# A hybrid decoder layer with a mixture of experts: a sixth expert buffer in shared tensors, the first experts' rows by dense one-hot products, and a new order of the front, the small products, the logits and the last loads

## The chip, the core and the metric

The kernel runs on one core of one Trainium2 chip. The engines used are TensorE (PE, matrix products; PEld is its weight load), VectorE (DVE), ScalarE (ACT), GpSimd (POOL) and SyncE (SP, which only issues transfers here). SBUF is the on-chip memory of 128 partitions, PSUM the eight accumulation banks that PE writes. The metric is the device time of one execution, in microseconds; the median of three runs is given, and one more execution was profiled.

## What is computed

One layer for 256 prompt tokens and 8 sequences of 8 sample tokens (320 tokens, D = 1024), all in fp32:

```python
xn = rmsnorm(x, norm1);  proj = xn @ w_in                      # 1024 x 7456
lru_x, lru_y, rw, gate_lru, gate_rwkv = split(proj)
out_lru  = rglru(causal_conv(lru_x)) * gelu(lru_y)
out_rwkv = rwkv7(rw, ...)                                      # 16 heads of 64
x = x + (sigmoid(gate_lru)*out_lru + sigmoid(gate_rwkv)*out_rwkv) @ w_out
t = rmsnorm(x, norm2)
g = argmax(t @ rg + rgb); two best of the 8 experts in group g # 32 experts
y = sum over the two: weight * (silu(t @ wg[e]) * (t @ wu[e])) @ wd[e]
out = rmsnorm(x + y, final_norm)
```

Each expert has three matrices of 1 MiB (gate, up, down: 1024 x 256 and 256 x 1024), so the experts' weights are 96 MiB. The states (convolution, LRU, token shift, WKV) are outputs too.

## The kernel before

Every engine has its own instruction stream, written out by hand; a wait on a counting semaphore stands wherever one engine needs another. There is no scheduler: the order on each engine is that of the code. The program has four stages.

**Front (0 to 65 us).** SP loads x, the states and the first weights; ACT issues 13 small vector loads into `vrows` (L1103), then squares and roots for the first norm. PE waits for all 13, transposes them (L582), transposes the states (`strows`, `shrows`, `murows`, 36 small transposes, L585 to L589), then the normed rows `xn` (24 transposes, L599, two banks in turn) and makes three products of the shared columns (L605). DVE scales the rows (L1402) and applies `norm1` by column (L1408).

**Pairs of heads (65 to 549 us).** `turn(i, ...)` runs eight times, six of them in a loop, once for each pair of heads (128 channels). The big projections are `proj` (L627); between them stand many small products of 64 rows or 64 columns: `own` (L667, L669), the transposes `turned` (L649: a plain product with the identity for the lower half, a transpose for the upper half), the samples' transposes (L697 to L705) and the levels of a triangular inverse (L738, L745). PE's last product of the first half of `proj(.. "r" ..)` waits for the DVE's first transposed level (`lvX`) and for ACT's copies (`tm`).

**Output projection and routing (549 to 619 us).** `out(t)` for three token tiles (L914), `x2(t)` transposes the rows normed with `norm2` (L932, L924), `logits(t)` (L956) multiplies by the router. DVE picks the experts (L1717 to L1784), PE counts places with triangular products (L972 to L977), DVE builds the one-hot `disp` for experts 0 and 1, and PE gathers their columns directly: for each of 8 chunks of D, `xn2` as weights and `disp` as moving operand (L983, L985). The rows of the other experts go through DRAM: `xn2d` is written by ACT's queue and gathered by POOL with indirect transfers (L533, L535).

**Experts (619 to 872 us) and the end.** For each expert e PE runs `up(e)` (`GU`, L1008, 64 slots), the transposes of the next rows (L1002), `dn(e-1)` (`DN`, L1015) and `turn_h(e)` (L1037). DVE copies the result to `ye`, POOL scatters it to `ybuf` in DRAM (L539). The weights go through five buffers, carved out of tensors whose earlier use has ended, so SP's loads wait: gate and up of experts 0 to 3, down of 0 go at once; down of 1 and gate and up of 4 after `out(2)` (`wo_ps` 3, since they lie over the weights of `out`); down of 3 after the logits; down of 2 and 4 after the first rows' products (`gT_ps` 2). From expert 5 on, SP waits for `gu >= e-4`, loads gate and up of e, waits for `dn >= e-4`, loads down of e. At the end SP loads the two choices of every token back from `ybuf` (`ya`, L505 to L509), DVE adds them with their weights (`combine`, L1840, L1841), and the last norm (ACT L1302, L1304, DVE L1704) is stored.

## Time and profile before

| | us |
|---|---|
| median of 3 runs | 897.65 (894.34 to 900.71) |
| profiled execution, its own time | 895.88 |
| its span | 894.1 |
| PE busy | 812.1 (91%) |
| DVE busy | 457.0 (51%) |
| ACT busy | 248.7 (28%) |
| moved by the DMA engines | 159.85 MB |

The page cuts the span in 40 slices of 22.35 us. Through the front and the pairs PE is at nine tenths and the DMA engines are mostly idle. From slice 25 on (559 us) the DMA engines run at nine tenths and about 390 GB/s, except in slice 27 (604 to 626 us), where they move 119 GB/s; TensorE's granted clock is down to a half in the same place. The chain that ended last is 70% PE, 10% transfers and 8% DVE.

### The profile page before, as it was taken

To read this page: it belongs to the slowest core of one execution; us is meant where nothing else is said; L and a number is where in the kernel's file an instruction comes from. 1 tells how busy PE (TensorE), PEld (TensorE's weight loads), DVE (VectorE), ACT (ScalarE), POOL (GpSimd) and SP (SyncE) were. 2 spreads that over 40 slices of the span, in tenths; PEclk is the share of its full clock that TensorE was granted. 3 is DMA by queue.
4 is the path that set the end of the run, shared out by engine and by line. 5 is a ranking of instruction groups with operands and counts; after the bars stand their busy time and mean duration, and the time that the engine had idled before them with its cause. 6 is when DMAs were issued, how large, how long until landed. Compare 5 with 4: busy or idle time off the path is not lost.

```text
span 894.1 us, 16251 instructions
## 1 busy us (share of the span) xinstructions
PE 812.1 (91%) x6152; PEld 510.3 (57%) x6152; DVE 457.0 (51%) x1065; ACT 248.7 (28%) x584; POOL 64.8 (7%) x72
## 2 busy tenths in 40 slices
PE   3999999999999999999999989979899988888780
PEld 3566666666666666666666655456555544445440
DVE  1376687686686786886875936143221111111114
ACT  4123342351441432433423523220111111111112
POOL 1000000000000000000000000000322222222110
PEclk9999999999999999999999999975999999999995
DMA  9252060060250140320600512993999999999955
GB/s 221 78 134 73 25 167 15 25 170 8 58 144 23 45 134 23 105 73 23 166 12 23 165 30 60 375 413 119 344 386 387 385 396 391 392 392 388 399 203 180
DMA packets 114225, 159.85 MB, mean 179 GB/s; under 512 B 27470, under 2 KB 91528, under 8 KB 105974
## 3 DMA queue, kind: packets, MB, share of 16 engines
q1 hardware_dynamic: 98180, 149.14, 48.6%
q0 software_dynamic: 5136, 6.04, 2.5%
q10 hardware_dynamic: 10867, 4.09, 1.9%
q8 instruction: 29, 0.48, 0.2%
q14 instruction: 13, 0.11, 0.0%
HBM read 155.99 MB, written 13.64 MB: 190 GB/s over the span
## 4 chain that ended last, share of the span: by engine, by line
PE 70%; DMA 10%; DVE 8%; SPq 7%; issue 3%; ACT 1%; ACTq 1%; DVEq 0%; POOLq 0%
PE bank L627 17%; PE bank L1008 7%; SPq L457 5%; PE bank L633 4%; PE bank L914 4%; PE bank L795 4%; PE bank L1015 3%; PE bank L858 3%; DMA scratch<-in_exp_up 3%; DMA wall<-in_exp_up 3%; PE bank L738 3%; DMA vecs<-in_exp_up 2%; PE bank L649 2%; PE bank L745 2%; DVE vecs L1465 2%
## 5 line engine op out<-in xcount | busy, mean ns | idle before, releaser
L627 PE MATMUL bank<-xnT,wall 128*128 128x320 f32 x656 | 195.3, 442 | 1.8 <-DVE wkv L1571 1.8
L627 PEld LDWEIGHTS bank<-xnT,wall 128*128 128x128 f32 x656 | 119.0, 190 | 51.5 <-DVE wkv L1571 5.4
L1813 DVE SCALAR_TENSOR_TENSOR vecs<-vecs,bank 128x128 f32<-128x128 f32 x32 | 9.2, 287 | 144.7 <-ACT vecs L1360 144.7
L1008 PE MATMUL bank<-vecs,scratch 128*64 128x256 f32 x448 | 56.5, 409 | 9.1 <-DMA vecs<-in_exp_up 8.2
L1008 PE MATMUL bank<-scratch 128*64 128x256 f32 x384 | 45.8, 393 | 11.8 <-DMA scratch<-in_exp_up 10.6
L1809 DVE COPY vecs<-bank 128x512 f32<-128x512 f32 x32 | 22.1, 691 | 58.1 <-PE bank L1015 42.3
L1008 PEld LDWEIGHTS bank<-vecs,scratch 128*64 128x64 f32 x448 | 33.5, 147 | 28.1 <-DMA vecs<-in_exp_up 9.6
L533 POOL DMA_INDIRECT merged<-xn2d,gidx x4 | 3.7, 918 | 622.5 <-DVE gidx L1791 621.6
L1360 ACT ACTIVATE vecs<-bank 128x128 f32<-128x128 f32 x32 | 8.9, 277 | 136.9 <-PE bank L1008 136.9
L795 PE MATMUL bank<-xnT,wall 128*128 128x320 f32 x128 | 43.9, 455 | 2.5 <-DVE wkv L1611 2.5
L1008 PEld LDWEIGHTS bank<-scratch 128*64 128x64 f32 x384 | 28.2, 141 | 25.9 <-DMA scratch<-in_exp_up 11.8
L1564 DVE TENSOR_TENSOR wkv<-bank,consts_sb 128x256 f32<-128x256 f32 (+1 forms) x40 | 18.1, 451 | 46.5 <-PE bank L738 46.5
L539 POOL DMA_INDIRECT ybuf<-vecs,sidx x32 | 32.1, 1004 | 77.6 <-DVE vecs L1809 76.9
L1002 PEld LDWEIGHTS bank<-consts_sb,merged 64*128 64x128 f32 x240 | 28.7, 200 | 12.0 <-issue 12.0
L858 PE MATMUL bank<-xnT,wall 128*128 128x320 f32 x112 | 33.1, 439 | 0.0
L1002 PE MATMUL bank<-consts_sb,merged 64*128 64x64 f32 x240 | 32.8, 277 | 0.0
L535 POOL DMA_INDIRECT merged<-xn2d,gidx x26 | 24.7, 949 | 108.0 <-PE bank L1002 104.8
L738 PEld LDWEIGHTS bank<-wkv,scratch 64*64 64x64 f32 x704 | 23.6, 134 | 14.7 <-issue 13.2
L914 PE MATMUL bank<-wall,merged 128*128 128x512 f32 (+1 forms) x84 | 30.7, 595 | 0.1
L738 PE MATMUL bank<-wkv,scratch 64*64 64x64 f32 x704 | 29.1, 224 | 0.9 <-DVE wkv L1571 0.9
L1008 PE MATMUL bank<-wall,scratch 128*64 128x256 f32 x192 | 23.7, 403 | 5.3 <-DMA wall<-in_exp_up 5.3
L795 PEld LDWEIGHTS bank<-xnT,wall 128*128 128x128 f32 x128 | 21.2, 190 | 10.8 <-DVE wkv L1611 4.8
(389 smaller groups left out, 1374.1 us busy)
## 6 DMA issues: line engine op xcount, KB each, us to landing
wall<-in_w_in SPq DMA_DIRECT2D x58, 512.0 KB, 5.6
vecs<-in_exp_gate SPq DMA_DIRECT2D x14, 1024.0 KB
vecs<-in_exp_up SPq DMA_DIRECT2D x14, 1024.0 KB
scratch<-in_exp_gate SPq DMA_DIRECT2D x12, 1024.0 KB
scratch<-in_exp_up SPq DMA_DIRECT2D x12, 1024.0 KB
scratch<-in_exp_down SPq DMA_DIRECT2D x7, 1024.0 KB
wall<-in_exp_down SPq DMA_DIRECT2D x7, 1024.0 KB
wall<-in_exp_gate SPq DMA_DIRECT2D x6, 1024.0 KB
```

What stands on the lines that cost most here:

```text
L457: sp.dma_start(wgu[b][:, g].rearrange("p k f -> p (k f)"), gu_src(name, e)).then_inc(S(f"ewg{b}"), 16)
L535: pool.indirect_dma_start(xg[j], None, xn2d, bass.IndirectOffsetOnAxis(ap=e, axis=0), bounds_check=last, oob_is_err=False).then_inc(S(sem) ...
L539: pool.indirect_dma_start(yhalf, bass.IndirectOffsetOnAxis(ap=e, axis=0), ye[:, b, :], None, bounds_check=4 * QROWS - 1, oob_is_err=False) ...
L627: q = mm(tpbank(L, name), wbuf[name][:, k, :], xnT[:, k, :], start=(k == 0), stop=(k == KC - 1))
L633: mm(tpbank(L, name), lhsT, rhs, start=True, stop=True).then_inc(S("tp"), 1)
L738: q = mm(bank[2][at64(e), 64 * u:64 * u + 64], am[at64(e), u, e, 0, :], X[at64(e), u, :], start=True, stop=True)
L795: q = mm(tpbank(L, "gr"), wbuf["gr"][:, k, :], xnT[:, k, :], start=(k == 0), stop=(k == KC - 1))
L858: q = mm(tpbank(L, "lx"), wbuf["lx"][:, k, :], xnT[:, k, :], start=(k == 0), stop=(k == KC - 1))
L914: q = mm(b, merged[:, k, t0:t0 + n], wo[k][:, 512 * h:512 * h + 512], start=(k == 0), stop=(k == KC - 1))
L1002: q = tr(b[:, CAP * k:CAP * k + CAP], src[:, k:D:KC], ident[r, r])
L1008: q = mm(b[64 * f:64 * f + 64, 0:256], xT[:, k, :], w[:, :, k, 128 * f:128 * f + 128], start=(k == 0), stop=(k == KC - 1))
L1015: q = mm(b[64 * d:64 * d + 64, :], hT[:, 64 * j:64 * j + 64], down(w, j, d), start=(j == 0), stop=(j == 1))
```

## The change

**Memory.** The small tensors that only the pairs of heads use (`s0raw`, `so_s`, `cvT`, `shT`, `w2a2`, `g2a`, `g2b`, `wxa`, the three `pad1`, `pad3`, `cacc`, `dif`) become slices of two tensors, `shared0` and `shared1`. After the last pair these hold gate and up of a sixth buffer. Its down matrix goes in three pieces to ends of `wall` and `wkv`. The gains of the last norm move to `scratch3` and are loaded when 28 experts' products are done.

**Loads.** Gate and up of expert 5 are issued before the wait for the first rows; `next_gu` runs one expert ahead of `next_dn`:

```diff
-            sp.dma_start(fnb, a["final_norm"].rearrange("(a d) -> a d", a=1).broadcast_to([P, D])).then_inc(S("fn_in"), 16)
-            sp.wait_ge(S("lg_ps"), 1)
+            sp.wait_ge(S("lg_ps"), 2)
             load_dn(3, 3)
+            sp.wait_ge(S("wkv_out"), 80 * PAIRS)
+            load_gu(5, 5)
             sp.wait_ge(S("xn2d"), 64)
-            sp.wait_ge(S("gT_ps"), 2)
+            sp.wait_ge(S("rows_ps"), 2)
             load_dn(2, 2)
             load_dn(4, 4)
...
-            for e in range(5, NE):
-                sp.wait_ge(S("gu"), e - 4)
-                load_gu(e % 5, e)
-                sp.wait_ge(S("dn"), e - 4)
-                load_dn(e % 5, e)
+            sp.wait_ge(S("rows_out"), 128)
+            load_dn(5, 5)
+            def next_gu(e):
+                sp.wait_ge(S("gu"), e - 5)
+                load_gu(e % 6, e)
+            def next_dn(e):
+                sp.wait_ge(S("dn"), e - 5)
+                load_dn(e % 6, e)
+            next_gu(6)
+            next_gu(7)
+            next_dn(6)
+            next_dn(7)
+            next_gu(8)
+            for e in range(9, NE):
+                next_gu(e)
+                next_dn(e - 1)
+            next_dn(NE - 1)
```

SyncE's expert loads from gate and up of expert 4 on, before ( `vecs`, `scratch`, `wall`, `xnT`, `wkv`, `merged` are the tensors that hold buffers):

```order
L457 DMA wall<-in_exp_gate 128x2048
L457 DMA wall<-in_exp_up 128x2048
L475 DMA wall<-in_final_norm 128x1024
L461 DMA xnT<-in_exp_down 128x2x1024
L461 DMA wkv<-in_exp_down 128x2x1024
L464 DMA wkv<-in_exp_down 128x1024
L464 DMA merged<-in_exp_down 128x512
L464 DMA xnT<-in_exp_down 128x512
L484 DMA wkv<-in_final_norm 64x512 x2
L457 DMA vecs<-in_exp_gate 128x2048
L457 DMA vecs<-in_exp_up 128x2048
L461 DMA scratch<-in_exp_down 128x2x1024
```

and the same place now:

```order
L491 DMA wall<-in_exp_gate 128x2048
L491 DMA wall<-in_exp_up 128x2048
L498 DMA xnT<-in_exp_down 128x2x1024
L494 DMA shared<-in_exp_gate 128x1024 x2
L494 DMA shared<-in_exp_up 128x1024 x2
L498 DMA wkv<-in_exp_down 128x2x1024
L501 DMA wkv<-in_exp_down 128x1024
L501 DMA merged<-in_exp_down 128x512
L501 DMA xnT<-in_exp_down 128x512
L501 DMA wall<-in_exp_down 128x1024
L501 DMA wkv<-in_exp_down 128x512 x2
L491 DMA vecs<-in_exp_gate 128x2048
```

The four pieces of expert 5 stand between down of 3 and down of 2, and 0.75 MiB of final gains is gone from here.

**First rows.** The rows of experts 0 and 1 are gathered as rows, with `disp` as weights and 512 columns of `xn2` moving, copied by ACT to `xg01`, and transposed:

```diff
-            for k in range(KC):
-                b, c = bank[0 if k < 4 else 3], 128 * (k % 4)
-                for t in range(2):
-                    mm(b[:, c:c + 128], xn2[:, t, k:D:KC], disp[:, t], start=(k % 4 == 0 and t == 0), stop=False, skip_group_check=True)
-                for h in range(2):
-                    q = mm(b[at64(h), c:c + 128], xn2h[at64(h), k:512:KC], disp[at64(h), 2], start=False, stop=True, skip_group_check=True)
+            for h in range(2):
+                b, c = bank[3 if h else 0], slice(512 * h, 512 * h + 512)
+                for t in range(2):
+                    mm(b[:], disp[:, t].rearrange("p e s -> p (e s)"), xn2[:, t, c], start=(t == 0), stop=False)
+                mm(b[:], disp[at64(h), 2].rearrange("p e s -> p (e s)"), xn2h[at64(h), :], start=False, stop=True).then_inc(S("rows_ps"), 1)
+            pe.wait_ge(S("rows_c"), 2)
+            for k in range(KC):
+                c = P * (k % 4)
+                q = tr(bank[1 if k < 4 else 4][:, c:c + P], xg01[:, k:D:KC], ident)
```

**Logits.** `norm2` is multiplied into the router's weights (`rw`), `x2` transposes `x1` itself, and DVE multiplies the logits by the inverse root afterwards. `logits(0)` and `logits(1)` stand around the second half of `out(2)`. TensorE from the third tile of `out` to the first expert's product, before:

```order
L914 MATMUL bank<-wall,merged 64x512 x14
L914 MATMUL bank<-vecs,merged 64x512 x2
L932 MATMUL bank<-consts_sb,wkv 128x128 x8
L939 MATMUL bank<-rowst,consts_sb 64x1 x2
L956 MATMUL bank<-rw,xnT 128x36 x8
L924 MATMUL bank<-consts_sb,wkv 128x128 x4
L956 MATMUL bank<-rw,xnT 128x36 x8
L956 MATMUL bank<-rw,xnT 64x36 x16
...
L983 MATMUL bank<-wkv 128x128 x2
L985 MATMUL bank<-wkv 64x128 x2
...
L1008 MATMUL bank<-vecs,scratch 64x256 x16
```

and now:

```order
L979 MATMUL bank<-wall,merged 64x512 x8
L998 MATMUL bank<-consts_sb,wkv 128x128 x8
L1023 MATMUL bank<-rw,xnT 128x36 x8
L979 MATMUL bank<-wall,merged 64x512 x6
L979 MATMUL bank<-vecs,merged 64x512 x2
L1023 MATMUL bank<-rw,xnT 128x36 x8
L990 MATMUL bank<-consts_sb,wkv 128x128 x4
...
L1051 MATMUL bank<-wkv 128x512 x2
L1052 MATMUL bank<-wkv 128x512
...
L1056 MATMUL bank<-consts_sb,merged 128x128 x8
L1080 MATMUL bank<-vecs,scratch 64x256 x16
```

Eight pairs of rows L983 and L985 became two pairs of L1051 and L1052 and eight transposes. The writes of `xn2d` are issued after the last root.

**Small products.** In `turn`, all of `own`'s first parts come first, then the quarter products grouped by bank; every `turned` is a plain product, in an order that alternates the output halves; the samples' transposes stand two products into `proj(.. "r" ..)`:

```diff
-                    for e in range(2):
-                        turned(b[at64(e), 128 * e:128 * e + 128], e, bk[:, 2 * j + e, 0], ident)
-                        turned(b[at64(1 - e), 128 * e:128 * e + 128], 1 - e, bk[:, 2 * j + e, 1], ident)
-                        turned(b[at64(1 - e), 384:512], 1 - e, vm[:, cols], ident)
+                    for e, x in ((0, 0), (0, 1), (1, 1), (0, 2), (1, 2), (1, 0)):
+                        rows = at64(e if x == 0 else 1 - e)
+                        src = vm[:, c0 + CH * e:c0 + CH * e + CH] if x == 2 else bk[:, 2 * j + e, x]
+                        mm(b[rows, 384:512] if x == 2 else b[rows, 128 * e:128 * e + 128], src, ident, start=True, stop=True)
...
+                    proj(L, i, "r", i + 1, 0, 2)
+                    samples()
+                    proj(L, i, "r", i + 1, 2, 4, akv_needs)
```

TensorE in a turn (L633 and L698 are `single`, L697 to L705 and L757 to L765 the samples' transposes), before:

```order
L649 MATMUL bank<-consts_sb,vecs 64x128 x6
L693 MATMUL bank<-consts_sb,wkv 128x128
L633 MATMUL bank<-wkv,w2a 128x320 x2
L649 MATMUL bank<-consts_sb,vecs 64x128 x6
L693 MATMUL bank<-consts_sb,wkv 128x128
L697 MATMUL bank<-consts_sb,vecs 64x64
L698 MATMUL bank<-consts_sb,vecs 64x64
L699 MATMUL bank<-consts_sb,wkv 64x64
```

and now:

```order
L750 MATMUL bank<-consts_sb,vecs 64x128 x6
L751 MATMUL bank<-consts_sb,wkv 128x128
L698 MATMUL bank<-wkv,shared 128x320 x2
L750 MATMUL bank<-consts_sb,vecs 64x128 x6
L751 MATMUL bank<-consts_sb,wkv 128x128
L692 MATMUL bank<-xnT,wall 128x320 x2
L757 MATMUL bank<-consts_sb,vecs 64x64
L758 MATMUL bank<-consts_sb,vecs 64x64
```

The number of small products is the same; two big ones (L692) moved ahead of the samples' transposes.

**Front.** Seven vector loads stay on ACT's queue, six go to POOL's, ahead of the router's. Each tile of x has its own semaphore. ACT takes square and root of a tile at once. The rows are no longer scaled: DVE makes a diagonal matrix `rstd` (128 x 128) of the inverse root, and PE's transposes of `xn` become products of `xt` with it, over four banks. The states' transposes (now with `norm2`) follow the second shared product.

```diff
-                    q = tr(b[:, c * P:c * P + n], xn[0:n, t, d:d + P], ident[0:n, 0:n])
+                    q = mm(b[:, c * P:c * P + n], xt[0:n, t, d:d + P], rstd[0:n, t, 0:n], start=True, stop=True)
```

**End.** All of choice 1 is loaded from `ybuf` before choice 2 and added for the three tiles, then choice 2; the root's table is loaded before the squares; the three last scalings stand after all additions.

## Rows read from the trace of the kernel before

**Rows 1.** The page: the span, and GB/s in 40 slices

```profile
span 894.1 us, 16251 instructions
...
GB/s 221 78 134 73 25 167 15 25 170 8 58 144 23 45 134 23 105 73 23 166 12 23 165 30 60 375 413 119 344 386 387 385 396 391 392 392 388 399 203 180
```

**Rows 2.** Windows: stretch, length, busy us by engine, granted clock, DMA share, GB/s

```profile
561.50:586.00 24.50, 24.50 (x86) 10.53 (x84) 5.46 (x8) 6.10 (x11) 0.00 (x0) 1.00 1.02 382
...
592.00:594.00 2.00, 2.00 (x34) 1.89 (x33) 0.00 (x0) 0.87 (x1) 0.00 (x0) 0.50 1.05 416
603.50:619.20 15.70, 14.91 (x67) 10.39 (x67) 6.51 (x25) 1.19 (x2) 0.00 (x0) 0.50 0.05 12
619.20:865.70 246.50, 219.68 (x1553) 123.64 (x1551) 40.35 (x104) 34.89 (x92) 58.52 (x60) 0.97 1.00 378
...
622.00:624.00 2.00, 2.00 (x20) 1.37 (x18) 0.00 (x0) 0.00 (x0) 0.00 (x0) 0.90 1.03 401
632.00:636.00 4.00, 2.96 (x16) 1.44 (x16) 0.19 (x1) 0.53 (x2) 0.00 (x0) 1.00 1.05 213
700.00:860.00 160.00, 136.79 (x939) 75.73 (x940) 24.58 (x59) 21.92 (x58) 34.27 (x35) 0.96 1.01 389
```

**Rows 3.** Timeline, output projection and routing: start, duration, engine, line, operands

```profile
564.25 12.18 PE L914 MATMUL bank<-wall,merged 128*128 128x512 f32 x28
...
586.08 0.38 SPq L461 DMA_DIRECT2D wall<-in_exp_down  x1
...
602.68 1.33 PE L983 MATMUL bank<-wkv 128*128 128x128 f32 x4 [0.93 <-DVE wkv L1752]
...
617.94 0.38 SPq L461 DMA_DIRECT2D wkv<-in_exp_down  x1
...
618.64 1.97 PE L1008 MATMUL bank<-vecs,scratch 128*64 128x256 f32 x8 [0.79 <-ACT scratch L1348]
...
624.19 0.33 SPq L457 DMA_DIRECT2D vecs<-in_exp_gate  x1
...
631.42 0.38 SPq L461 DMA_DIRECT2D scratch<-in_exp_down  x1
```

**Rows 4.** Chain that ended last, experts: start, duration, what

```profile
702.75 3.60 PE bank L1008 x32
...
709.51 3.60 PE bank L1008 x32
...
863.02 3.67 PE bank L1008 x32
...
869.10 1.96 PE bank L1015 x8
```

**Rows 5.** Timeline, one turn of the loop

```profile
256.23 1.41 PE L649 MATMUL bank<-consts_sb,vecs 128*64 128x128 f32 x9
...
261.01 2.32 PE L627 MATMUL bank<-xnT,wall 128*128 128x320 f32 x8
...
261.25 0.51 DVE L1553 STREAM_TRANSPOSE wkv<-wkv 128x320 f32<-128x320 f32 x1
...
293.33 0.66 PE L813 MATMUL bank<-wkv 128*64 128x128 f32 x8
```

**Rows 6.** Front: a piece of the chain, then the timeline

```profile
6.41 8.22 DMA vrows<-in_rwkv_ln_b
...
19.03 4.69 PE L599 MATMUL bank<-consts_sb,scratch 128*128 128x128 f32 x20
...
25.78 0.34 PEld L605 LDWEIGHTS bank<-xnT,wall 128*128 128x128 f32 x1 [0.20 <-issue]
...
28.45 6.68 PEld L605 LDWEIGHTS bank<-xnT,wall 128*128 128x128 f32 x25 [0.20 <-issue]
```

**Rows 7.** Timeline, the first and the last of VectorE's work after the last scatter

```profile
879.78 1.28 DVE L1840 SCALAR_TENSOR_TENSOR wkv<-wall,r,wkv 128x1024 f32<-128x1024 f32 x1 [7.22 <-DMA scratch<-ybuf]
...
889.93 0.75 DVE L1704 SCALAR_TENSOR_TENSOR wkv<-wkv,rowst 128x512 f32<-128x512 f32 x1
```

361 lines of the change are left out of this document (211 added, 150 removed).

## The prediction, written before the changed kernel was run

> **What bounds the kernel now.** I read the page first: the span is 894.1 us, and the moved bytes per slice show two halves, a quiet one up to slice 24 and a full one from slice 25 on, with one hole at 119 GB/s [rows 1]. The windows then say what each part is worth. From 700 to 860 us the DMA engines are busy all the time and move 389 GB/s, while PE is busy 137 of 160 us: the experts are bound by the transfers [rows 2]. The chain gives both paces: the products L1008 of two neighbouring experts start 6.76 us apart while the buffers are full (702.75, 709.51), but expert 31's start at 863.02, so 18 further experts took 8.53 us each [rows 4]. PE would need 6.76. So from routing on only four things count: when the stream of weights begins, how many bytes it has, how long it stands idle, and what follows its last byte. It stands idle from 603.5 to 619.2 us, with a share of 0.05 [rows 2]. The timeline says why: SP issues down of experts 2 and 4 at 617.94, when PE's first-row products are done, and these began at 602.68 [rows 3]. Everything else has been loaded by then.
>
> Before routing the bound is PE. A microsecond saved on PE in the pairs of heads shifts all that follows, unless another engine is just behind it.
>
> **Part 1: first rows.** Before, 602.68 to 617.94: 15.3 us. Now six products of 512 columns, in fp32 two records each. `out`'s 28 records of that width took 12.18 us, 0.435 us each, at the full clock (2.4 GHz) [rows 3]. But the clock is at its lower level (1.2 GHz, granted 0.50) from 592 on, when PE did narrow logits and then waited, and through all of 603.5 to 619.2, narrow products back to back; it came up in 622 to 624 (granted 0.90 there), about 3.6 us after L1008's wide products began at 618.64 [rows 2, 3]. I take the same here: 3.6 us at 0.87 us a record are 4.1 records, the other 7.9 take 3.4 us, 7.0 in sum. All at the lower level 10.4, all at the full one 5.2. `rows_ps` 2 then comes at 609.7 instead of 617.9, and since SP's issue at 617.94 filled the engines at 619.2, the stream runs again at 611.0: **8.2 us earlier** (bounds 4.8 and 10). The Trainium skill (TensorE: Matmul & The Clock Gate, What's actually happening) says the same in words: throttled is the default, activity releases it. It gives this sum no number.
>
> Are the loads ahead of it done by then? `wo_ps` 3 now follows `x2(1)` and `logits(0)` on PE, about 3 us later, so down of 1 and gate and up of 4, issued at 586.08 before [rows 3], come at 589.0 and flow at 590.3. What was left at 586 (17.5 us until 603.5, at the 0.416 MB/us of 592 to 594, less the 5.75 MiB issued later, leave 1.2 MiB) is gone at 589.0, so there is a new hole of 1.3 us; then 6 MiB of weights and 1.25 of `xn2d` take 18.3 us, until 608.6 (estimates from [rows 2, 3]). That is before 611.0. The hole costs nothing in the forecast case.
>
> **Part 2: sixth buffer and moved gains.** From 619.2 to 865.7 before: 83.25 MiB in 246.5 us, 2.96 us per MiB, with the gathers and scatters in it [rows 2]. Now 2 MiB of expert 5 lie in the former hole and 0.25 MiB of gains at the end: 2.25 x 2.96 = **6.7 us**. Bounds: 2.25 MiB at 389 GB/s alone are 6.1, and 6.7. The pieces are 4 KB per partition instead of 8 KB; down's rows are 4 KB too and lie in the same 389 GB/s.
>
> **Part 3: order of the loads.** In 632 to 636 the stream moved 213 GB/s instead of 389: 1.8 us lost, because down of 5, issued at 631.42, had waited for `dn` and held gate and up of 6 behind it [rows 2, 3]. Now 3 MiB of down matrices (8 us) cover expert 0, whose gate and up free at its products' end: after 609.7 two copies at the 0.7 us from 617.94 to 618.64 [rows 3], eight transposes at half of a two-record product's 0.235 [rows 6], 2.4 in sum, then 3.7 us of products [rows 4]; and two experts' gates come ahead of the downs. I credit **1 us** of the 1.8 (bounds 1.8, and a loss of 1.5 if transposes and products run at the lower clock). At the end of the stream, gate and up of 31 stand before down of 30 and 31, instead of only before down of 31. Before, expert 31's products began at 863.02 and its second product at 869.10, 3.4 us after the stream's end at 865.7 [rows 2, 4]. Now its first products begin some 5.4 us before that end, and the 6.1 us chain from there to the second product ends 0.7 after it: **2.7 us** (bounds 0 and 3.4).
>
> **Part 4: end.** VectorE works from 879.78, when both choices of tile 0 have landed, to 890.68 [rows 7], with 9.9 us of work (six times 1.28 and three times 0.75) in these 10.9. Choice 1 of tile 0 is one 512 KB transfer (1.3 us at 0.4 MB/us) ahead of choice 2, the work is the same: **1.6 us** (0 to 2.3). The root's table load and the squares were hidden behind VectorE and stay so.
>
> **Part 5: small products.** Six `turned` cost 1.41 us as nine records; eight records of the form that they now all have, 128 rows by 64 columns with 128 moving, in alternating halves, took 0.66 us [rows 5]. Twelve are 0.99: 0.42 saved, twice a turn, 0.84. The regrouped `own` may add 0.3, not counted. What covers it: PE reaches the last product of the first half of `r` (261.01 plus six records of 0.29, 262.7) and needs VectorE's transposed level there, which ends at 261.76 [rows 5]. That leaves 0.8 us with the semaphore; VectorE works without a break from PE's last y of the turn before, so beyond 0.8 it is the bound and the wait only changes its name. The samples' transposes, moved past two big products, keep PE from waiting for `am`; the two come back in the same half, so they cost nothing. Eight turns: **6.4 us** (0 to 7).
>
> **Part 6: front, a loss.** The last of ACT's 13 vector loads was issued at 6.41 and took 8.22 us; PE then transposed vectors and states until 19.03 and the normed rows after that [rows 6]. Now the seventh of ACT's loads is the last, six fewer at about 0.4 us each: issued at 4.0, it lands at 12.3 if it takes as long. POOL's six have a queue of their own, not shown in this trace. Between 9.6 (a landing time of two thirds) and 14.6 I take 12. Then 24 products stand for 24 transposes, in two records each: 20 records took 4.69 us [rows 6], 0.235 each, so 32 wide ones and 16 of half size take 9.4 us at least, and up to 12.8 at the pace of L983's products, 1.9 us for four wide and two pairs of half ones. I take 11. With 0.7 for the vectors' transpose and its copies the shared products then start at 23.7 instead of 25.1 (two records before the weight load at 25.8) [rows 6]. The states' 36 transposes, 3.8 us before, now stand between the shared products and cost PE between 1.9 and 3.8, I take 2.8. Net **-1.4 us** (from +4 to -6).
>
> **Sum.** 8.2 + 6.7 + 1 + 2.7 + 1.6 + 6.4 - 1.4 = 25.2 us. The profiled execution took 895.88 us, 1.8 below the median of 897.65; the sum is made against it: 870.7 us. `logits` ahead of the norm costs and brings nothing: PE has the same products, its end moves by some 0.2 us, and VectorE's `scale(2)` runs behind the last logits.
>
> **Rivals.**
> - *The clock stays down through the first rows.* For it: narrow products did not raise it in 15 us [rows 2]. Against: these are four times as wide. Then 10.4 us, the stream 3.4 us later, a bubble behind expert 0 of 1.5: 875.6 us.
> - *The small products do not overlap*, or VectorE takes it all back. Against: the 0.66 us row. 877.1 us.
> - *The front gains.* The weight loads of L605 are 0.53 us apart at 25.8 and 0.267 from 28.45 on (25 in 6.68 us) [rows 6]: PE ran at half pace until there, also through the transposes, though the window column shows 1.00 so early. If products wake the clock where transposes did not, the front is some 5 us shorter than in the forecast: 866 us. The Trainium skill has this as a rule (TensorE: Matmul & The Clock Gate, PE-mode transpose: transposes do not count as activity); by that rule, this rival holds.
> - *The front loses much more*, because a wide product costs as four transposes: 24 x 4 records at 0.235 are 22.6 us, 11.6 above my 11: 882 us. Against: `out`'s records are 0.435 for 512 columns, so products go by columns [rows 3]. The Trainium skill's same page (Terms) calls the transpose mode four times as fast for fp32; by that alone this rival would hold.
> - *The sixth buffer does nothing*, because PE, not the stream, limits the experts once it starts late. Then parts 2 and 3 and the hole bring nothing, and parts 1, 4, 5, 6 leave 14.8: 881 us. Against: PE's own pace from 613.5 on puts expert 31 at 826 (31 x 6.76 and 3 more), long before its weights.
> - *Slower than before: the clock.* The stream hides PE only while an expert costs PE less than the stream's time. Of the 6.76 us, L1008 and L1015 are 5.5 [rows 4], which double at the lower clock: 12.2. Each wait for data risks a fall, and the change adds some. PE then puts expert 31 at 613.5 + 31 p. All of the gain is gone where that is 869.6, 6.6 behind 863.0 (what the end and the pairs still save): p = 8.26, the lower level for 27% of the time. At 35% p is 8.69 and the time 909 us. Against: the granted clock of 0.96 over 700 to 860 is the lower level for 8% [rows 2].
>
> **How the numbers follow.** Forecast case 0.62; clock down in the first rows 0.10; no gain in the small products 0.09; front gains 0.09; front loses much 0.02; buffer without effect 0.02; slower by the clock 0.03; the rest, 0.03, is a change that nearly cancels. The predicted time is the forecast's, 871 us. The range from 862 to 880 takes in the first three rivals and the bounds of part 6. A run's spread is some 3 us either way of the median, so about 1% is what a measurement can tell from no change: under 888.7 is faster. Faster 0.94, same 0.03, slower 0.03.
>
> **What would show it.** First rows: the records of L1051 and L1052 take 7 us and the granted clock rises within them. Stream: the share stays near 1 from 561 on, but for a hole of 1 to 2 us near 589 and 2 to 3 at 609 to 611 (less what the pairs of heads saved). Turn: a turn of the loop is 0.8 us shorter and PE waits a little for VectorE's transposed level. Front: the first shared product starts at 23.7. End: the 31.1 us from expert 31's first product (863.0) to the span's end become about 29.5 (the tail's 1.6 less), and more only if the last down matrix is late. The prediction is wrong if the hole moves elsewhere (the gate of expert 6, the gathers of expert 2), or if PE's pace per expert exceeds 8.5 us.

## The result, and the profile after

| | before | after |
|---|---|---|
| median of the timed runs, us | 899.18 (894.34 to 900.97, 4 runs) | 871.90 (871.51 to 873.74, 4 runs) |
| profiled execution, its own time | 895.88 | 871.51 |
| its span | 894.1 | 869.7 |

The ratio is 0.9716, with a 95% interval of 0.9684 to 0.9747: the change makes the kernel faster by 27 us in the medians and by 24.4 in the profiled spans. The time forecast was 871. The total is right; as the parts show, it is right partly because two errors cancel.

The page of the kernel after, its span and the moved bytes in 40 slices of 21.7 us:

```profile
span 869.7 us, 16331 instructions
...
GB/s 220 137 139 25 25 173 14 30 176 5 58 147 24 39 144 24 81 102 24 130 54 24 159 41 37 317 358 378 322 379 385 387 384 382 397 389 386 387 281 188
```

The slice at 119 GB/s in [rows 1] is gone. One at 322 is left, in slice 28 counted from 0 (609 to 630 us).

The timeline of PE after, front, routing and first expert (start, duration, engine, line, operands, count of records, idle time before and what ended it):

```profile
10.71 0.45 PE L641 MATMUL bank<-consts_sb,vrows 128*128 128x128 f32 x1 [10.71 <-DMA vrows<-in_rwkv_ln_b]
10.95 7.48 PE L651 MATMUL bank<-scratch 128*128 128x128 f32 x48
18.95 8.88 PE L668 MATMUL bank<-xnT,wall 128*128 128x320 f32 x32 [0.52 <-DVE xnT L1488]
...
30.16 4.49 PE L668 MATMUL bank<-xnT,wall 128*32 128x320 f32 x16
34.59 4.57 PE L692 MATMUL bank<-xnT,wall 128*128 128x320 f32 x16
...
591.74 3.60 PE L1051 MATMUL bank<-wkv 128*128 128x512 f32 x4 [0.93 <-DVE wkv L1855]
595.26 1.12 PE L1052 MATMUL bank<-wkv 64*128 64x512 f32 x2
596.32 1.98 PE L1051 MATMUL bank<-wkv 128*128 128x512 f32 x4
598.23 1.12 PE L1052 MATMUL bank<-wkv 64*128 64x512 f32 x2
...
602.02 5.25 PE L1080 MATMUL bank<-vecs,scratch 128*64 128x256 f32 x32 [0.82 <-ACT scratch L1423]
```

The first four of the wide first-row records take 0.9 us each, the later ones 0.50 to 0.56: PE's clock came up inside them. Expert 0's products then run partly at the lower level again (granted 0.50 from 602 to 604; 5.25 us, where a later expert's take 3.67).

Five marks cut both executions in five stretches. Before they are PE's first `r` product (39.99), its first product of `out` (549.54), SP's issue of down behind the first rows (617.94), expert 31's first product (863.02) and the end (894.1) [rows 1, 3, 4]. After they are 34.59, 539.67, 599.43, 839.57 and 869.7.

| stretch | before | after | saved | forecast |
|---|---|---|---|---|
| front | 39.99 | 34.59 | 5.4 | -1.4 |
| pairs of heads | 509.55 | 505.08 | 4.5 | 6.4 |
| output projection to first rows done | 68.40 | 59.76 | 8.6 | 8.2 |
| from there to expert 31's weights | 245.08 | 240.14 | 4.9 | 10.4 (6.7 + 1 + 2.7) |
| expert 31 to the end | 31.08 | 30.13 | 1.0 | 1.6 |
| sum | 894.1 | 869.7 | 24.4 | 25.2 |

The front brought 6.8 us more than forecast, the stream of weights 5.5 less.

### The profile page after: what moved, and what is told of

Read it like the earlier page. It is cut to its first block, busy times and chain, and to the rows that moved or that the text cites. A ratio compares the mean times of both kernels' runs of the same rounds, so it can differ in the third digit from the quotient of the medians.

```text
span 869.7 us, 16331 instructions
## 1 busy us (share of the span) xinstructions
PE 793.1 (91%) x6180; PEld 496.0 (57%) x6180; DVE 456.9 (53%) x1069; ACT 249.7 (29%) x587; POOL 68.2 (8%) x78
## 4 chain that ended last, share of the span: by engine, by line
PE 55%; DVE 19%; SPq 10%; DMA 8%; issue 4%; ACT 1%; DVEq 1%; POOL 0%; POOLq 0%; ACTq 0%
PE bank L692 14%; PE bank L1080 7%; SPq L491 5%; PE bank L979 4%; PE bank L860 4%; DMA wall<-in_exp_up 3%; PE bank L1087 3%; PE bank L798 3%; SPq L501 3%; PE bank L698 2%; DMA vecs<-in_exp_up 2%; PE bank L805 2%; DVE vecs L1607 2%; DVE vecs L1556 2%; DVE vecs L1579 2%
## 5 line engine op out<-in xcount | busy, mean ns | idle before, releaser
L692 PE MATMUL bank<-xnT,wall 128*128 128x320 f32 x656 | 198.6, 444 | 4.9 <-DVE wkv L1662 1.9
L692 PEld LDWEIGHTS bank<-xnT,wall 128*128 128x128 f32 x656 | 118.0, 189 | 55.6 <-DVE wkv L1662 5.4
L1080 PE MATMUL bank<-vecs,scratch 128*64 128x256 f32 x384 | 47.4, 403 | 7.8 <-DMA vecs<-in_exp_up 7.0
L860 PE MATMUL bank<-xnT,wall 128*128 128x320 f32 x128 | 43.9, 455 | 2.5 <-DVE wkv L1702 2.5
L1197 ACT ACTIVATE shared<-bank 128x256 f32<-128x256 f32 x32 | 12.4, 386 | 112.5 <-PE bank L692 106.7
L1080 PE MATMUL bank<-scratch 128*64 128x256 f32 x320 | 36.7, 382 | 7.0 <-DMA scratch<-in_exp_up 5.9
L1080 PEld LDWEIGHTS bank<-vecs,scratch 128*64 128x64 f32 x384 | 28.3, 145 | 23.2 <-DMA vecs<-in_exp_up 8.1
L923 PE MATMUL bank<-xnT,wall 128*128 128x320 f32 x112 | 33.1, 439 | 0.0
L1080 PEld LDWEIGHTS bank<-scratch 128*64 128x64 f32 x320 | 22.9, 137 | 17.8 <-DMA scratch<-in_exp_up 6.6
L805 PEld LDWEIGHTS bank<-wkv 64*64 64x64 f32 x576 | 19.3, 134 | 14.2 <-issue 12.7
```

The lines of the kernel that those rows point to most:

```text
L692: q = mm(tpbank(L, name), wbuf[name][:, k, :], xnT[:, k, :], start=(k == 0), stop=(k == KC - 1))
L805: q = mm(bank[3][at64(e), 64 * u:64 * u + 64], Y[at64(e), u, :], W[at64(e), u, :], start=True, stop=True)
L860: q = mm(tpbank(L, "gr"), wbuf["gr"][:, k, :], xnT[:, k, :], start=(k == 0), stop=(k == KC - 1))
L923: q = mm(tpbank(L, "lx"), wbuf["lx"][:, k, :], xnT[:, k, :], start=(k == 0), stop=(k == KC - 1))
L1080: q = mm(b[64 * f:64 * f + 64, 0:256], xT[:, k, :], gate_up(w, k)[:, :, 128 * f:128 * f + 128], start=(k == 0), stop=(k == KC - 1))
```

## Experiments

Each is the changed kernel with one thing altered. Its own profiled execution is cut by the same marks, so that small differences can be seen that the medians of runs alone would leave open. How far to trust such a cut shows in stretches that an experiment left alone. From SP's issue behind the first rows to expert 31's first product it took 240.1 to 240.3 us in the five executions with the same loads and expert 0's products at 5.2 to 5.4 us; the end, with the same instructions, took 29.95 to 30.7, once 31.0.

### The first rows as before

```diff
+ for k in range(KC):          # 8 chunks of D, xn2 as weights, disp moving, as before
-     mm(b[:], disp[:, t]..., xn2[:, t, c], ...)      # and no copy, no transposes behind
- sp.wait_ge(S("rows_ps"), 2)
+ sp.wait_ge(S("gT_ps"), 2)
```

> The changed kernel with the rows of experts 0 and 1 made by the former 32 narrow products straight into the transposed form, without the copy and the transposes; everything else, the sixth buffer too, is as in the changed kernel, and down of 2, 4 and 5 wait for these products' end. Theory A (the first rows' end sets the time of the stream's restart, and the stream sets the end): the products take 15.3 us instead of 7.6, down of 2 is issued near 607 instead of 599.4, and the whole is 7 to 8 us longer (about 879.5). Theory B (in the changed kernel PE or the gathers set the start of the experts): under 4 us longer, since this way has no copies and transposes behind it.

Measured: 880.06 us, 8.2 above the changed kernel (ratio to before 0.9812, 0.9779 to 0.9846). The products ran from 591.43 to 606.62. Theory A holds: what is saved on them moves the stream's restart (606.70 for 599.43), and the restart moves the end by about the same (7.0 us between the two profiled spans).

### Expert 5's gate and up behind the first rows

```diff
- sp.wait_ge(S("wkv_out"), 80 * PAIRS)
- load_gu(5, 5)
  sp.wait_ge(S("rows_ps"), 2)
  load_dn(2, 2)
  load_dn(4, 4)
+ sp.wait_ge(S("wkv_out"), 80 * PAIRS)
+ load_gu(5, 5)
```

> The changed kernel with gate and up of expert 5 issued behind down of 2 and 4, after the first rows, instead of ahead of them; the sixth buffer is there, but 2 MiB no longer go into the time in which the stream waits. Theory A (transfers bound the experts, 2.96 us per MiB): the DMA engines stand idle from about 594 to 600 and the whole is 5.5 to 6 us longer (about 877.6). Theory B (something other than bytes sets the first experts' time): under 3 us longer.

Measured: 877.40 us, 5.5 more. From SP's issue at 599.62 to expert 31's weights at 844.48 it took 244.9 us, 4.7 more than in the changed kernel. Theory A holds, with 2.4 us per MiB in the stretch and 2.8 in the medians instead of 2.96. The room for a sixth expert pays because its gate and up can be loaded this early.

### The last loads in the former order

```diff
- for e in range(9, NE):
+ for e in range(9, NE - 1):
      next_gu(e)
      next_dn(e - 1)
+ next_dn(NE - 2)
+ next_gu(NE - 1)
  next_dn(NE - 1)
```

> The changed kernel with down of expert 30 issued ahead of gate and up of 31 again, as before the change. In the changed kernel expert 31's products start at 839.6, when its up matrix has landed. Theory A (the prediction's: transfers are served in the order of issue, so 1 MiB more lies ahead of up of 31): they start 2.7 us later, and the whole is 2.5 us longer (about 874.4). Theory B (several transfers are under way together and the 16 engines end them at different times, so the last order of issues moves little): under 1 us longer.

Measured: 877.93 us, 6.0 more, which neither theory has. SP's issue behind the first rows is at 598.83 and expert 31's products start at 841.76: 242.9 us, 2.8 more, where theory A has 2.7. The rest is in the timeline of PE and the windows of that kernel (stretch, length, busy us by engine, granted clock, DMA share, GB/s):

```profile
841.76 6.23 PE L1082 MATMUL bank<-vecs,scratch 128*64 128x256 f32 x32 [4.52 <-DMA vecs<-in_exp_up]
```

```profile
838.00:840.00 2.00, 0.00 (x0) 0.00 (x0) 0.00 (x0) 0.00 (x0) 0.98 (x1) 1.00 0.66 265
842.00:846.00 4.00, 4.00 (x20) 2.18 (x20) 0.00 (x0) 0.00 (x0) 0.00 (x0) 0.50 0.24 93
```

PE has waited 4.5 us for the weights, the granted clock has gone to 0.50, and the 32 records take 6.23 us instead of 3.67. They are on the path, so a wait that is 2.8 us longer costs 5.4 here. The two profiled spans differ by 4.7 (the first rows ended 0.6 earlier in this one), the medians by 6.0. The forecast priced the first half only.

### All loads in the former order

```diff
- next_gu(6); next_gu(7); next_dn(6); next_dn(7); next_gu(8)
- for e in range(9, NE): next_gu(e); next_dn(e - 1)
- next_dn(NE - 1)
+ for e in range(6, NE): next_gu(e); next_dn(e)
```

> The changed kernel with each expert's gate, up and down issued in one piece from expert 6 to 31, as the former kernel did from 5 on, the end included. In the changed kernel the stretch from 12 to 28 us behind the first rows' end moves 296 GB/s, before the change 337. Theory A (the prediction's: the new order saves about 1 us at the start and 2.7 at the end): 3.7 us longer (about 875.6). Theory B (the low rate belongs to POOL's gathers, the order of the loads does nothing for it): the stretch moves 290 to 310 GB/s or, with a down matrix that holds back the next gate, somewhat less, and the whole is within 1 us of the kernel with the old end alone.

Measured: 874.25 us, 2.4 more than the changed kernel. From 600.70 to expert 31's products at 843.32 it took 242.6 us, 0.3 less than with the old end alone, and the clock did not fall ahead of them (30.3 us from there to the end). So the new order of the first loads is worth nothing, or costs 0.3; the stretch from 12 to 28 us moved 326 GB/s, more than the changed kernel's 296. Neither theory holds as it was written. Theory A had 3.7 us, of which 1 for the start. Theory B had the whole within 1 us of the kernel with the old end alone, and it is 3.7 below that (874.25 for 877.93), since the fall of the clock is missing; only its stretch agrees. Theory B also had the rate at 290 to 310 at most.

### Plain loads for the first four gathers

```diff
- pool.indirect_dma_start(xg[j], None, xn2d, bass.IndirectOffsetOnAxis(ap=e, axis=0))
+ pool.dma_start(xg[j], xn2d[0:CAP, :])
```

> The changed kernel with the first four of POOL's gathers (experts 2 to 5) as plain loads of the same size from the same buffer, rows 0 to 63, so these experts' values are wrong. In the changed kernel the stream moves 274 GB/s from 614 to 628 instead of some 390, which costs 4.1 us; before the change 260 GB/s from 630 to 636, or 2.0 us. Theory A (the indirect gathers occupy the DMA engines at a low rate, up to 39% of their time for 1 MB in 10 us): with plain loads the stretch moves over 370 GB/s and the whole is 3 to 4 us shorter (about 868). Theory B (the order of the loads leaves too few transfers to fill the engines): no change. Theory C (any transfer of such rows beside the weights costs as much): no change, and POOL's queue takes as large a share as before.

Measured: 873.05 us (870.09 to 876.8), not distinguishable from the changed kernel; from 602.15 to 841.46 it took 239.3 us, 0.8 less, and the second piece, from 12 to 28 us, moved 318 GB/s instead of 296. POOL's queue in the kernel after, then here (queue: packets, MB, share of the time of 16 engines), in the first 10 and 6 us of these transfers:

```profile
q1 hardware_dynamic: 233, 1.65, 61.5%
q0 software_dynamic: 299, 1.00, 39.4%
```

```profile
q0 software_dynamic: 203, 0.70, 53.3%
q1 hardware_dynamic: 179, 1.21, 51.0%
```

1.00 MB took 3.9 us of all engines by index and 0.70 MB took 3.2 without, so per byte the plain loads are no cheaper. Theory C holds in the main: the 3 to 4 us of theory A are not there. The 0.8 us is more than the unchanged stretch differs between executions (0.2), so it may be what the index costs.

### Wide products in PE's idle time around routing

```diff
  logits(2)
+ for _ in range(7): mm(bank[2][:, 0:256], ident, ident (256 columns))
  pe.wait_ge(S("Mk"), 1)
  # and one such product behind the counts, the first rows and their transposes
```

> The changed kernel with wide products of the unit matrix (256 columns, seven behind the last logits, one each behind the counts, the first rows and their transposes) in PE's idle time around routing; nothing uses their result. In the changed kernel the granted clock is 0.50 from 585 to 595.3 and from 602.1 to 605.6, the first-row products take 7.6 us and expert 0's first 32 records 5.25 instead of 3.67. Theory A (idle time and narrow work before them make the clock fall, wide work holds it): the first-row products take 5.9 us or less and expert 0's 3.7; the stream restarts 1.7 us earlier and the whole is 1.5 to 2 us shorter (about 870). Theory B (seven products are not enough to hold it): the first-row products take 7.6 us as before, and the counts may start up to 0.5 us later; no gain.

Measured: 871.17 us (870.9 to 872.42), 0.7 less, which the spread does not separate from the changed kernel. The windows of this kernel, at the seven products, at the counts and at the first-row products:

```profile
583.50:586.80 3.30, 3.30 (x19) 2.58 (x15) 2.83 (x15) 1.28 (x1) 0.00 (x0) 1.00 1.01 372
588.50:591.80 3.30, 3.26 (x14) 2.48 (x14) 1.23 (x7) 0.31 (x2) 0.00 (x0) 0.57 1.01 400
592.00:595.50 3.50, 3.50 (x5) 1.00 (x4) 3.02 (x15) 0.00 (x0) 0.00 (x0) 0.50 1.04 414
```

The seven products keep the clock up while they run, but PE then waits 1.7 us and does the narrow counts, and it is down again ahead of the first rows, which take 7.9 us. Expert 0's products do take 3.67 us now instead of 5.25, and that gained 1.5 us in the stream: from SP's issue at 599.82 to expert 31's products at 838.47 it took 238.65 us for 240.14. SP's load of expert 6's gate waits for expert 0's products, and its issue stands 6.3 us behind the one at 599.82 here, against 7.9 in the changed kernel. Here, then in the changed kernel:

```profile
606.12 0.33 SPq L491 DMA_DIRECT2D vecs<-in_exp_gate  x1
```

```profile
607.30 0.33 SPq L491 DMA_DIRECT2D vecs<-in_exp_gate  x1
```

Two other executions had expert 0 at the full level by themselves (3.67 us), those of the kernels with transposes between the wide products and with the small products as before; there the stretch took 238.56 and 238.85. The 1.5 us does not show in the span of this execution (869.5 for 869.7), since its first rows ended 0.4 later and its end took 31.0 us instead of 30.1, with more waiting for the loads of the two choices.

### One queue for the vectors

```diff
- for name, key in VECTORS[7:]: pool.dma_start(...)   # vec_late
- for name, key in VECTORS[:7]: act.dma_start(...)
+ for name, key in VECTORS: act.dma_start(...)
```

> The changed kernel with all 13 vector loads on ScalarE's queue, in the new order. Theory A (the vectors' landing sets PE's start, and the second queue brings it forward): the last vector lands near 14.6 us as before the change instead of 10.6, PE's first transpose follows, and the whole is 4.0 us longer than the changed kernel (about 876). Theory B (the landing is set by what SyncE's loads leave free, not by the queues): the landing moves by under 1 us.

Measured: 874.12 us, 2.2 more. The timeline of PE, its first transpose:

```profile
12.60 0.45 PE L638 MATMUL bank<-consts_sb,vrows 128*128 128x128 f32 x1 [12.60 <-DMA vrows<-in_rwkv_ln_b]
```

Before the change this transpose stands at 14.77, after it at 10.71. So the second queue is worth 1.9 us of the 4.1; the other 2.2 come from something else in the new front's loads (their order on SP and ACT is a candidate, and wasn't tried).

### Transposes instead of products in the front

```diff
- q = mm(b[...], xt[0:n, t, d:d + P], rstd[0:n, t, 0:n], start=True, stop=True)
+ q = tr(b[...], xt[0:n, t, d:d + P], ident[0:n, 0:n])
```

> The changed kernel, but the 24 front products of the rows with the scaled unit matrix are transposes of the rows with the plain unit matrix (the scaling by 1/rms is left out, so the values differ). In the changed kernel the 24 products run from 10.95 us, the shared products from 18.95 to 27.8, and all the first 32 records of L668 take 8.9 us. Theory A (products raise PE's granted clock, transposes do not): the 24 transposes take 24 x 0.235 = 5.6 us or a little more, the shared products start near 17, but their first 32 records take about 10.5 us instead of 8.9, since the first 3 to 4 us of them go at half pace; they end near 27.5, and the whole time stays within 1 us of the changed kernel. Theory B (any work of PE raises the clock, or time alone does): the transposes come up to full pace after 3 to 4 us, the first shared product starts near 15 and 32 records take 8.9; the front and the whole are 3 to 4 us shorter.

Measured: 871.52 us (867.08 to 873.62), as the changed kernel. PE in this front:

```profile
10.99 3.82 PE L651 MATMUL bank<-consts_sb,scratch 128*128 128x128 f32 x24
15.78 8.88 PE L668 MATMUL bank<-xnT,wall 128*128 128x320 f32 x32 [0.97 <-DVE xnT L1488]
...
26.98 6.18 PE L668 MATMUL bank<-xnT,wall 128*32 128x320 f32 x16
33.09 4.58 PE L692 MATMUL bank<-xnT,wall 128*128 128x320 f32 x16
```

Theory A falls. Up to 14.81 PE had done transposes only, 0.159 us each, and the 32 records behind them take 8.88 us, the full pace from the first one. So products are not needed for the clock to be up; whether the transposes raised it or time alone did, this run doesn't separate. The shared products start 3.2 us earlier than in the changed kernel, as theory B says; half of that is lost again at 26.98, where 16 records take 6.18 us instead of 4.49. By the rule of the Trainium skill (TensorE: Matmul & The Clock Gate, PE-mode transpose) transposes do not count as activity for the clock. This trace does not agree, and the measurement decides. The kernel before is what the rule would give: transposes only up to 24.6, and half pace until 28.4. What makes these two differ was not isolated.

### Wide products ahead of the front

```diff
  pe.wait_ge(S("first_in"), 16)
+ for _ in range(6): mm(bank[1][:], ident, ident (512 columns))
  pe.wait_ge(S("vec_in"), 16 * 7)
```

> The changed kernel with six products of 512 columns of the unit matrix on PE ahead of the vectors' transpose, while PE has nothing to do; their result is used by nothing. Theory A (the clock is low at the start because PE has done no products, and they raise it): the granted pace of the 24 front products is full from their first one; they take about 5.5 us instead of 8.0, and the whole is about 2 us shorter than the changed kernel (870). Theory B (VectorE's scaling and evictions set that stretch): the front is shorter by under 0.5 us.

Measured: 874.46 us, 2.6 more. PE in this front:

```profile
5.00 7.07 PE L640 MATMUL bank<-consts_sb 128*128 128x512 f32 x12 [5.00 <-DMA consts_sb<-in_consts]
11.91 0.27 PE L643 MATMUL bank<-consts_sb,vrows 128*128 128x128 f32 x1
12.02 5.66 PE L653 MATMUL bank<-scratch 128*128 128x128 f32 x48
18.20 10.57 PE L670 MATMUL bank<-xnT,wall 128*128 128x320 f32 x32 [0.52 <-DVE xnT L1490]
```

The front products do take 5.66 us instead of 7.48. But the added ones start later than I had them and end 1.2 us behind the vectors' landing, and the clock falls twice behind them: 10.57 us instead of 8.88 here, 6.18 instead of 4.49 behind the states. A clock that was up early did not stay up. That the added products cause the two falls is not shown, since a front without them had both as well (the small products as before, below).

### Narrow transposes between wide products

```diff
  for k in range(KC):
      q = mm(bank[5 + j][0:w, 0:N], wbuf[n][:, k, 0:w], xnT[:, k, :], ...)
+     for one in small_ones[5 * k:5 * k + 5] if n == "ly" else []:
+         one()
- if n == "ly":
-     states()
```

> The changed kernel with the 36 narrow transposes of states between the eight products of ly, five behind each, instead of in one piece behind them. In five of ten profiled executions with the changed front the products behind that piece took 6.2 us instead of 4.5, because the granted clock had fallen to 0.50 by then. Theory A (the piece of narrow work makes the clock fall): no such fall here; the first r product starts at 34.6 or earlier in this execution too, and the median of the timed runs is 0.5 to 1.5 us below the changed kernel. Theory B (the fall comes whatever stands there): the fall appears in the same place, or the median does not move.

Measured: 875.96 us (872.85 to 877.41), 4.1 more. (The expectation counts five of ten; it was four of nine by then.) In the profile the clock stays up: the last 16 records take 4.50 us. But each change between the wide products and a group of five costs some 0.3 us, so that shared products and states together take 17.6 us instead of 15.6. The median lies above that, and why is open. As a cure it failed, and one execution without a fall does not show that theory A is right, since most executions have none.

### The small products of a turn as before

```diff
- for u in range(5): own(u, 0)
- for us in ((0, 2), (1, 3), (4,)): ...
- for e, x in ((0, 0), (0, 1), (1, 1), (0, 2), (1, 2), (1, 0)): mm(..., src, ident)
+ for j in range(2): for part in range(3): ...          # own, as before
+ turned(...)                                            # half of them transposes, as before
```

> The changed kernel with the order and form of the small products of a turn (own, and the two groups of turned ones, half of them transposes) as they were before the change; the samples' transposes stay moved. Theory A (as the prediction has it, the two groups cost 0.4 us less each and nothing else matters): a turn takes 62.6 us again instead of 61.9, the whole is 5 to 6 us longer than the changed kernel. Theory B (the moved samples' transposes saved the time, since PE no longer waits for the masked products): a turn stays under 62.1 us.

Measured: 879.33 us, 7.4 more. The same products of two turns in a row are 62.7 us apart (190.28, 253.00), in the changed kernel 61.9 (184.12, 246.07). From the first `r` product to `out` it took 511.0 us for 505.1. Theory A holds: 0.8 us a turn, 5.9 in sum. Some 4.2 us of this profiled execution are something else: its front is the changed kernel's, instruction by instruction, but two falls of the clock stand in it, and its first-row products took 10.2 us for 7.7. The 7.4 of the medians is above theory A's 5 to 6, and what the rest is stays open.

```profile
10.91 8.32 PE L651 MATMUL bank<-scratch 128*128 128x128 f32 x48
19.75 10.57 PE L668 MATMUL bank<-xnT,wall 128*128 128x320 f32 x32 [0.52 <-DVE xnT L1495]
...
32.65 6.18 PE L668 MATMUL bank<-xnT,wall 128*32 128x320 f32 x16
38.77 4.57 PE L692 MATMUL bank<-xnT,wall 128*128 128x320 f32 x16
```

### The end in the former order

```diff
- for q in range(2): for t in range(2): ya[q][:, t, :] ...
+ for t in range(2): for q in range(2): ya[q][:, t, :] ...
- for t in range(3): combine(0, t)      # then combine(1, t), then the scalings
+ for t in range(3): combine(0, t); combine(1, t); inverse(t - 1); scale(t - 1)
```

> The changed kernel with the former end: choices 1 and 2 of each tile loaded together and VectorE's additions and scalings in the former order (the root's table is still loaded early). In the changed kernel 30.1 us pass from expert 31's first product to the end of the span, before the change 31.1. Theory A (prediction: choice 1 first is worth 1.6): 31.7 us. Theory B (half of it is lost again, since the six loads of the new order come later one behind the other and VectorE waits some 0.3 us ahead of each of four additions): 30.7 to 31.1 us, the whole 0.6 to 1 us longer.

Measured: 872.99 us (868.82 to 880.01), which the spread hides. From expert 31's first product (839.79) to the end (870.2) it took 30.4 us, 0.3 more than in the changed kernel, where theory A has 1.6 more and theory B 0.6 to 1. Since the unchanged end differs by more than that between executions, the order of the loads is worth little here, and nothing is shown to be gained by it. What is clear of it is the first addition: VectorE waits 5.95 us for it here and 6.10 in the changed kernel, against 7.22 before [rows 7]. So that gain comes with either order; each addition now waits for its own choice only, and that this is the reason is argued from the code.

## Why the prediction was right, and where it was not

**First rows: right.** 8.6 us for 8.2. The products took 7.6 us for the forecast's 7.0, with the clock rising 3.6 us into them, as supposed from expert 0 of before. A point that I had put at nothing brought 1.1: from `out`'s start to the first-row products it took 53.1 us before and takes 52.1. Some 0.8 of it is the clock: the last 48 narrow records of the logits took 3.94 us before, where the granted clock went to 0.50 at 592 [rows 2], and take 1.98 and 1.13 now at 1.00. That this comes from the new place of the logits was not tested.

**Loads ahead of them: right.** The new hole is there, in a window of the kernel after (the columns as above):

```profile
578.00:580.50 2.50, 2.50 (x20) 1.66 (x16) 0.69 (x1) 0.67 (x2) 0.00 (x0) 1.00 0.25 62
```

The forecast had it at 589.0 to 590.3; all of this lies 9.9 us earlier now, and the hole is somewhat longer. It cost nothing, but the margin is used up: the forecast had the early loads done 2.4 us ahead of the restart, and here they moved until 599.7, when SP had just issued the next ones (599.43). First rows that are faster still could bring only what is idle between 599.8 and 600.6.

**Bytes, sixth buffer and moved gains: right in kind, somewhat too large.** The run without the early load puts it at 4.7 us in the stretch and 5.5 in the medians, for 2 MiB that I had at 5.9. The 0.7 us for the gains was not tested; they are issued at 825.85 now, behind expert 31's up matrix (821.16), and take 14.2 us to land, so part of them still moves ahead of its products.

**Order of the loads: one half right, one wrong.** The end was right (2.8 for 2.7). The 1 us at the start fell. Two steps failed. One is that expert 0's products run at the full level: they took 5.25 us, not 3.7. Such a fall was in my bounds; it cost 1.5 us (below). The other is the reading of 632 to 636 in [rows 2]: I put its 213 GB/s down to a down matrix that waited and held the next loads behind it. The queues of the kernel before in that window say what moved:

```profile
q0 software_dynamic: 228, 0.73, 90.1%
q1 hardware_dynamic: 29, 0.12, 14.8%
```

POOL's first four gathers had 90% of the engines' time for 0.73 MB, that is 0.2 MB/us. They are not a hole that an order of loads could fill, and in the kernel after they run side by side with the weights over a longer time. There the weights beside them were slow as well: 1.65 MB in 6.2 us of all engines, 0.27 MB/us, for 0.39 over the whole stream. The windows of the kernel before and after, from the first rows' end on, in pieces of 12, 16 and 32 us:

```profile
617.94:629.94 12.00, 10.94 (x93) 7.05 (x95) 1.71 (x9) 1.28 (x4) 2.74 (x3) 0.81 0.93 339
629.94:645.94 16.00, 13.73 (x102) 8.68 (x99) 3.25 (x13) 2.19 (x6) 4.88 (x6) 1.00 1.02 337
645.94:677.94 32.00, 32.00 (x233) 17.85 (x234) 6.29 (x15) 5.48 (x14) 9.71 (x10) 1.00 1.03 381
```

```profile
599.43:611.43 12.00, 10.57 (x94) 7.51 (x96) 1.71 (x10) 1.92 (x4) 1.41 (x2) 0.86 0.91 348
611.43:627.43 16.00, 12.47 (x87) 7.26 (x85) 3.54 (x13) 2.36 (x7) 5.40 (x7) 1.00 1.01 296
627.43:659.43 32.00, 32.00 (x233) 17.96 (x229) 5.64 (x14) 5.49 (x14) 9.66 (x10) 1.00 1.02 379
```

In the second piece 16 us at 41 GB/s less are 0.66 MB, 1.7 us at 389 GB/s. The share of busy engines is 1.01: nothing is idle, the same busy time just moves less.

**What is missing of the stream's 5.5 us.** Three parts can be named. The start of the order gave nothing (1). The second piece costs 1.7, and most of that comes back where expert 0's products run at the full level. In the kernel with wide products around routing the first two pieces are

```profile
599.82:611.82 12.00, 11.19 (x103) 7.69 (x105) 1.75 (x9) 2.37 (x6) 2.68 (x3) 1.00 0.95 359
611.82:627.82 16.00, 13.95 (x103) 8.81 (x100) 3.41 (x13) 2.19 (x6) 4.96 (x6) 1.00 1.02 328
```

and the whole stretch was 1.5 us shorter, in this execution and two others, than in the five with expert 0 at 5.2 to 5.4 us. The third part is in the bytes of the weights' queue from the first rows to expert 31's products, before (619 to 862) and after (601 to 839):

```profile
q1 hardware_dynamic: 16693, 86.96, 92.4%
```

```profile
q1 hardware_dynamic: 18044, 84.52, 93.4%
```

Expert 31's first products need 82.25 MiB (86.24 MB) before and 79 MiB (82.84 MB) after; 0.7 and 1.7 MB more have moved by then. That 1.0 MB, 2.5 us, belongs to transfers issued behind the awaited ones, the last down matrices and the gains, which share the engines with the last gate and up. This sum comes to 5.2 of 5.5. Its first part was tested by a run of its own, the second rests on eight executions that differ in expert 0's clock, and the third is argued from the counts. The higher rate of the second piece does not reach the end by itself: with all loads in the former order it moved 326 GB/s, and the stretch was only 0.3 shorter than with the old end alone. Why the gathers and the weights move less side by side stays open.

**End: too large.** 1.0 for 1.6. VectorE's first addition comes 6.1 us behind the last scatter's start instead of 7.2 (forecast: 1.3 us earlier). But then it waits three times for a load:

```profile
856.90 1.95 DVE L1943 SCALAR_TENSOR_TENSOR wkv<-wall,r,wkv 128x1024 f32<-128x1024 f32 x2 [0.39 <-DMA wall<-ybuf]
859.17 1.28 DVE L1943 SCALAR_TENSOR_TENSOR wkv<-scratch,r,wkv 128x1024 f32<-128x1024 f32 x1 [0.33 <-DMA scratch<-ybuf]
860.72 1.95 DVE L1943 SCALAR_TENSOR_TENSOR wkv<-scratch,r,wkv 128x1024 f32<-128x1024 f32 x2 [0.26 <-DMA scratch<-ybuf]
```

That is 1.0 us, and its work takes 11.1 us from first to last instead of 10.9 [rows 7]. The 1.6 had it close up by 0.3 instead. Since the same end takes 29.95 to 30.7 us in other executions, the 1.0 itself is uncertain by half a microsecond.

**Small products: right by the turn, wrong in the count.** 0.69 a turn in the profile, 0.8 by the run with the old ones, for 0.8. But 4.5 in sum for 6.4: I multiplied by eight turns. The first two `own` groups are 62.55 us apart for 62.69 before, and the last turn's way to `out` takes 45.9 us in both, so six turns save 0.7 and two nothing. In the first turn PE waits for ACT instead:

```profile
66.42 1.34 PE L692 MATMUL bank<-xnT,wall 128*128 128x320 f32 x4 [1.18 <-ACT vecs L1247]
```

**Front: wrong in sign.** 5.4 us saved for a loss of 1.4. Three terms of the sum were too dear: the vectors land at 10.7 (I took 12 between 9.6 and 14.6), the 24 products take 8.0 with their last eviction (I took 11, having 0.235 us a record from [rows 6]; transposes took 0.159 in the run that has them), and the states cost 2.4 (2.8). The fourth is the 1.6 us by which 48 shared records are faster (8.88 and 4.49 instead of 14.98), because the clock is up already. That was the rival *the front gains*, and its result came true (5 us better than the forecast). Its reason did not: the front with transposes has the clock up as early. What kept it down until 28.4 in the kernel before, with 36 narrow transposes and waits between the others, was not isolated.

**The other rivals.** The clock was not down through the first rows; the buffer has its effect; 24 wide products took 7.48 us and 24 transposes 3.82, so a product costs two transposes, not four; and PE did not set the stream's pace: where it was busy all the time (627 to 659), the DMA share was 1.02 as well. The kernel with the old end shows a small piece of the clock rival, though: a wait for weights that grows by 2.8 us can cost 5.4.

No version that was run beats the changed kernel by more than the spread; the one with wide products around routing (871.17) is 0.7 below it, within the spread, though its stream is 1.5 us shorter.

## What to carry to other kernels

When the DMA engines' share is full and the rate is low, ask which queue has the time before blaming the order of the loads: gathers of 4 KB rows took one and a half times to twice the engine time per byte of the weights. Take the time per instruction for a sum from a place where the clock's level is known, and count for which turns of a loop a saving can reach the path, since the first and the last have other neighbours. Before calling a change without effect because the total stands still, look at the stretch that it touches: the faster expert 0 was worth 1.5 us there. A forecast that lands on the total still has to be checked stretch by stretch; here 6.8 us too little and 5.5 too much nearly cancelled.

## What the runs showed of the hardware

- The same front, unchanged, ran its shared products with PE's clock up throughout, or with one or two falls; each fall costs 1.7 us (32 records in 10.57 instead of 8.88, 16 in 6.18 instead of 4.49). It happened behind the narrow transposes in four of the twelve fronts that have them in one piece, two of these with other work ahead. One or two such falls are as large as the spread of the timed runs; that they are its cause is not shown.
- The clock was up behind transposes alone: 25 of them in 4.1 us, and full pace behind them.
- Expert 0's products at 5.2 to 5.4 us instead of 3.67 made the stream behind them 1.5 us longer (240.1 to 240.3 us in five executions, 238.6 to 238.9 in three).
- A wait of 4.5 us ahead of expert 31's products put them at the lower level (6.23 us for 3.67); one of 1.3 us, and one of 1.9 with the former order of all loads, did not.
- 0.73 MB of gathers took 3.6 us of all 16 engines, 0.70 MB of plain loads of as many rows 3.2.
